# Row sums on quarters of the PE array, seven ring slots, and one kept weight chunk per layer

## The reference

```python
q = (xb @ w_query).reshape(PEER_BLOCK, PEER_HEADS, 2, D_HALF)
s = jnp.einsum('thpd,hpkd->thpk', q, sub_keys)
sv, si = lax.top_k(s, TOPK_HALF)                       # 16 best keys on each side
cand = sv[:, :, 0, :, None] + sv[:, :, 1, None, :]
cv, ci = lax.top_k(cand.reshape(...), TOPK)            # 16 best pairs
idx = i1 * N_KEYS + i2
g = jax.nn.softmax(cv, axis=-1)
a = jax.nn.gelu(jnp.einsum('thkd,td->thk', expert_u[idx], xb))
return jnp.einsum('thk,thkd->td', g * a, expert_v[idx])
```

## Time and profile before

| | |
|---|---|
| median of 3 runs | 1833.76 us |
| the profiled execution | 1834.33 us |
| its span, first to last instruction | 1832.5 us |
| mean granted TensorE clock | 0.967 |
| PE busy | 1557.9 us, 85% |
| DVE busy | 1268.3 us, 69% |
| POOL busy | 654.4 us, 36% |
| ACT busy | 287.1 us, 16% |
| DMA | 735.00 MB, mean 401 GB/s |
| chain that ended last | PE 44%, DMA 38%, DVE 8%, issue 7% |

### The profile page before, as it was taken

The page is one execution under the profiler, slowest core; times in us unless marked ns, Lnnn a source line. Parts: engine busy times, 40 slices in busy tenths (PEclk is TensorE's granted clock), DMA queues, the critical chain, the costliest instruction groups (busy, mean ns, idle before and its releaser), DMA issues.

```text
span 1832.5 us, 17962 instructions
## 1 busy us (share of the span) xinstructions
PE 1557.9 (85%) x5880; PEld 852.7 (47%) x5880; DVE 1268.3 (69%) x3220; ACT 287.1 (16%) x959; POOL 654.4 (36%) x580
## 2 busy tenths in 40 slices
PE   7987999998967999987778799989877778777776
PEld 6984566654823765642221177547423222222211
DVE  1338667867779667678887646676888976565565
ACT  1112131103112111111111111031111110000010
POOL 0012333334333233334444333353544443434441
PEclk9998999998988999999999999999999999999999
DMA  8779999999999999999999999999999999999996
GB/s 342 283 264 422 377 395 418 388 415 420 418 416 399 421 421 421 421 421 420 419 403 384 421 421 421 421 411 421 406 421 408 420 422 421 421 422 415 416 415 251
DMA packets 103536, 735.00 MB, mean 401 GB/s; under 512 B 12337, under 2 KB 12849, under 8 KB 14962
## 3 DMA queue, kind: packets, MB, share of 16 engines
q0 software_dynamic: 82944, 604.02, 80.1%
q1 hardware_dynamic: 19730, 127.92, 17.4%
q10 hardware_dynamic: 768, 1.91, 0.3%
HBM read 732.28 MB, written 1.52 MB: 400 GB/s over the span
## 4 chain that ended last, share of the span: by engine, by line
PE 44%; DMA 38%; DVE 8%; issue 7%; DVEq 2%; POOL 1%; ACT 1%; ACTq 0%; POOLq 0%
DMA uvring<-expert_uv_dram,idx 36%; PE psum L598 22%; PE psum L608 12%; PE psum L712 4%; PE psum L640 3%; DVE diag L1101 1%; DVE uvring L1088 1%; PE psum L616 1%; POOL uvring L565 1%; DMA arena<-ln_bias_dram 1%; DMA wring<-w_chunks_dram 1%; PE psum L733 1%; PE psum L692 1%; PE psum L695 1%; PE psum L630 0%
## 5 line engine op out<-in xcount | busy, mean ns | idle before, releaser
L598 PE MATMUL psum<-uvring,diag 128*128 128x512 f32 (+1 forms) x2160 | 1056.4, 626 | 250.7 <-DVE diag L1101 241.7
L565 POOL DMA_INDIRECT uvring<-expert_uv_dram,idx x576 | 654.2, 1136 | 1152.1 <-PE psum L598 967.9
L1088 DVE SCALAR_TENSOR_TENSOR uvring<-uvring,xn 128x1024 f32<-128x1024 f32 x576 | 705.1, 1224 | 377.2 <-DMA uvring<-expert_uv_dram,idx 365.6
L598 PEld LDWEIGHTS psum<-uvring,diag 128*128 128x128 f32 (+1 forms) x2160 | 375.3, 187 | 855.2 <-DVE diag L1101 482.8
L608 PEld LDWEIGHTS psum<-xT,wring 128*128 128x128 f32 x2304 | 296.6, 193 | 30.0 <-issue 28.4
L608 PE MATMUL psum<-xT,wring 128*128 128x160 f32 (+1 forms) x2304 | 300.2, 289 | 0.9 <-ACT xT L781 0.7
L844 ACT ACTIVATE a_gelu<-a_raw 128x1 f32<-128x1 f32 x576 | 114.8, 202 | 1169.9 <-DVE uvring L1088 1169.3
L1101 DVE TENSOR_SCALAR diag<-ident,a_gelu,gate 128x128 f32<-128x128 f32 x476 | 163.6, 344 | 34.6 <-ACT a_gelu L844 34.6
L763 ACT ACTIVATE arena<-psum 128x128 f32<-128x128 f32 (+2 forms) x164 | 48.6, 306 | 268.3 <-PE psum L608 177.4
L712 PE MATMUL psum<-wring,arena 128*128 128x256 f32 x384 | 88.1, 385 | 1.0 <-issue 0.8
L712 PEld LDWEIGHTS psum<-wring,arena 128*128 128x128 f32 x384 | 72.8, 192 | 18.7 <-issue 8.8
(11 more groups left out here) (93 smaller groups left out, 666.0 us busy)
## 6 DMA issues: line engine op xcount, KB each, us to landing
wring<-w_chunks_dram SPq DMA_DIRECT2D x106, 1024.0 KB
uvring<-expert_uv_dram,idx POOLq DMA_INDIRECT x576
uvring<-w_chunks_dram SPq DMA_DIRECT2D x6, 1024.0 KB, 12.5
gain<-gains_dram SPq DMA_DIRECT2D x4, 512.0 KB, 11.7
x<-x_tok_dram SPq DMA_DIRECT2D x2, 512.0 KB, 4.9
uvring<-ln_gain_dram SPq DMA_DIRECT2D x1, 1024.0 KB, 25.0
uvring<-ln_bias_dram SPq DMA_DIRECT2D x1, 1024.0 KB, 27.7
keys<-sub_keys_dram SPq DMA_DIRECT2D x2, 512.0 KB, 7.2
```

The source lines that it names most:

```text
L565: pool.indirect_dma_start(uvring[:, n % RING, :], None, expert_uv, bass.IndirectOffsetOnAxis(ap=idx[t][:, i:i + 1], axis=0),).then_inc(uv_ ...
L598: mm = nc.tensor.matmul(acc[0:r, c * 512:(c + 1) * 512], diag[:, place % DIAGS, 0:r], uvring[:, n % RING, D + c * 512:D + (c + 1) * 512], ...
L1088: nc.vector.scalar_tensor_tensor(out=uvring[:, slot, 0:D], in0=uvring[:, slot, 0:D], scalar=1.0, in1=xn[t][:, :], op0=ALU.mult, op1=ALU.mu ...
```

## The change

Row sums. For tiles 0 and 1 the product of a 128x128 diagonal with 128x512 becomes four products per item of 64x64 with 64x512: partition half i of the diagonal and of the v row, column half c, output on partition half j of bank i. Each of the four touches another quarter of the PE array. The diagonal is stored 64 wide (`twin`, made once, has the identity's two diagonal blocks side by side on the partitions). For tile 2 it is four products of 128x32 with 256 columns each, outputs on four strips of 32 partitions. `acc` then has half of the result on the wrong partitions, so at a tile's end a new ACT step, `turn_sum`, copies these parts to `turned` on the right ones, and `add_sum` adds from there.

Items on DVE. `ON_VECTOR` is empty; all 576 items go through PE.

Buffers. `RING` goes from 8 to 7. A new buffer `kept` holds the first chunk of each layer from the first pass to the second, so that it isn't loaded again; the other chunks go through `wring` as before. Five chunks instead of six lie in the expert ring at the start.

```diff
+KEEP = 1
+EARLY = KEEP + 5
+RINGED = [n for n in range(EARLY, PASS_CHUNK0[-1]) if n - max(p for p in PASS_CHUNK0 if p <= n) >= KEEP]
-RING = 8
+RING = 7
-ON_VECTOR = {(0, 0): (32, 128, (2, 6, 10, 14)), (1, 0): (0, 64, (3, 8, 13))}
+ON_VECTOR = {}
...
+                if c < KEEP:
+                    if n == PASS_CHUNK0[2] + c:
+                        unused(PASS_CHUNK0[1] + c)
+                        sp.dma_start(kept[:, c, :, :], w_chunks[LAYER_CHUNK0[1] + c]).then_inc(kept_landed[c], 16)
+                    return
...
-                for c in range(2):
-                    mm = nc.tensor.matmul(acc[0:r, c * 512:(c + 1) * 512], diag[:, place % DIAGS, 0:r],
-                                          uvring[:, n % RING, D + c * 512:D + (c + 1) * 512],
-                                          start=(n == mine[0]), stop=(n == mine[-1]))
+                if t == 2:
+                    for q in range(4):
+                        mm = nc.tensor.matmul(acc[32 * q:32 * q + 32, 0:256], diag[:, place % DIAGS, 0:32],
+                                              row[:, D + 256 * q:D + 256 * (q + 1)], start=first, stop=last)
+                else:
+                    for c in range(2):
+                        for i in range(2):
+                            j = i if c == 0 else 1 - i
+                            mm = nc.tensor.matmul(acc[64 * j:64 * j + 64, 512 * i:512 * (i + 1)],
+                                                  diag[64 * i:64 * i + 64, place % DIAGS, :],
+                                                  row[64 * i:64 * i + 64, D + 512 * c:D + 512 * (c + 1)],
+                                                  start=first, stop=last)
...
+            def turn_sum(l, t):
+                act.wait_ge(v_tensor, RANK[TENSOR_ITEMS[l, t][-1]] + 1)
+                if list(END).index((l, t)):
+                    act.wait_ge(acc_read, list(END).index((l, t)))
+                if t == 2:
+                    for q in range(1, 4):
+                        done = nc.scalar.copy(turned[0:32, 256 * (q - 1):256 * q], acc[32 * q:32 * q + 32, 0:256])
+                else:
+                    nc.scalar.copy(turned[0:64, 0:512], acc[64:P, 0:512])
+                    done = nc.scalar.copy(turned[64:P, 0:512], acc[0:64, 512:D])
+                done.then_inc(acc_turned, 1)
...
-                did(nc.vector.tensor_tensor(x[t][0:r, 0:512], x[t][0:r, 0:512], acc[0:r, 0:512], ALU.add))
-                nc.vector.tensor_tensor(x[t][0:r, 512:D], x[t][0:r, 512:D], acc[0:r, 512:D], ALU.add
+                if t == 2:
+                    did(nc.vector.tensor_tensor(x[2][0:32, 0:256], x[2][0:32, 0:256], acc[0:32, 0:256], ALU.add))
+                else:
+                    for i in range(2):
+                        rows = slice(64 * i, 64 * i + 64)
+                        did(nc.vector.tensor_tensor(x[t][rows, 0:512], x[t][rows, 0:512],
+                                                    acc[rows, 512 * i:512 * (i + 1)], ALU.add))
+                dve.wait_ge(acc_turned, list(END).index((l, t)) + 1)
+                r, s = (slice(0, 32), slice(256, D)) if t == 2 else (slice(0, P), slice(512, D))
+                nc.vector.tensor_tensor(x[t][r, s], x[t][r, s], turned[r, 0:D - s.start], ALU.add
                                         ).then_inc(acc_read, 1)
```

More of the change, by code:

```diff
@@ L464, in trunk @@
         w_landed = [sem(f"w_landed{r}") for r in range(WRING)]
-        early_landed = [sem(f"early_landed{c}") for c in range(EARLY)]
+        early_landed = [sem(f"early_landed{c}") for c in range(EARLY - KEEP)]
+        kept_landed = [sem(f"kept_landed{c}") for c in range(KEEP)]
         part_used = sem("part_used")
@@ L478, in trunk @@
         v_tensor, v_vector, acc_read = sem("v_tensor"), sem("v_vector"), sem("acc_read")
+        acc_turned = sem("acc_turned")
         y_ready, conv_ready = sem("y_ready"), sem("conv_ready")
@@ L485, in early_chunk @@
         def early_chunk(c):
-            return uvring[:, 2 + c, :].rearrange("p (k c) -> p k c", k=KD)
+            return uvring[:, 2 + c - KEEP, :].rearrange("p (k c) -> p k c", k=KD)
         def wait_group(e, key):
@@ L501, in load_chunk, with unused @@
                 l = 0 if n < PASS_CHUNK0[2] else 1
-                c, r = n - max(p for p in PASS_CHUNK0 if p <= n), n - EARLY
-                if r >= WRING:
-                    kind, what = CHUNK_AFTER[n - WRING]
+                c = n - max(p for p in PASS_CHUNK0 if p <= n)
+                def unused(m):
+                    kind, what = CHUNK_AFTER[m]
                     if kind == "part":
@@ L512, in _ @@
             sp.dma_start(ident[:, :], ident_c).then_inc(ident_landed, 16)
-            for c in range(EARLY):
-                sp.dma_start(early_chunk(c), w_chunks[c]).then_inc(early_landed[c], 16)
+            for c in range(KEEP):
+                sp.dma_start(kept[:, c, :, :], w_chunks[c]).then_inc(kept_landed[c], 16)
+            for c in range(KEEP, EARLY):
+                sp.dma_start(early_chunk(c), w_chunks[c]).then_inc(early_landed[c - KEEP], 16)
             for n in range(EARLY, EARLY + WRING):
@@ L581, in chunk @@
             def chunk(n, c):
+                if c < KEEP:
+                    pe.wait_ge(kept_landed[c], 16 * (n // 2 + 1))
+                    return kept[:, c, :, :]
                 c += PASS_CHUNK0[n]
                 if c < EARLY:
-                    pe.wait_ge(early_landed[c], 16)
+                    pe.wait_ge(early_landed[c - KEEP], 16)
                     return early_chunk(c)
-                r = c - EARLY
+                r = RINGED.index(c)
                 pe.wait_ge(w_landed[r % WRING], 16 * (r // WRING + 1))
@@ L592, in weigh @@
                 l, t, _ = ITEMS[n]
-                mine, place, r = TENSOR_ITEMS[l, t], RANK[n], 32 if t == 2 else P
+                mine, place = TENSOR_ITEMS[l, t], RANK[n]
+                first, last, row = n == mine[0], n == mine[-1], uvring[:, n % RING, :]
                 if n == mine[0] and (l, t) != (0, 0):
@@ L852, in _ @@
                     gelu(2 * p + 1)
+                for lt, end in END.items():
+                    if p == end + 1:
+                        turn_sum(*lt)
                 for k in PLAN["ACT"].get(p, []):
@@ L1138, in _ @@
             dve.wait_ge(const_landed, 16 * N_CONST)
+            after(did(nc.vector.tensor_tensor(twin[:, :], ident[:, 0:64], ident[:, 64:P], ALU.add)))
             for p in range(TURNS):
```

17 lines of the change are left out of this document (11 added, 6 removed).

## The result

The changed kernel takes 1820.94 us (median of 4 runs, 1820.36 to 1821.85), the kernel before 1832.78 (4 runs, 1831.26 to 1833.84). The ratio is 0.9939, 95% interval 0.9924 to 0.9955: 11.8 us faster, where 9.2 had been forecast. The profiled execution took 1821.85 us, its span is 1820.0.

The account below looks back on a forecast made before the run. DMA was taken to bound the kernel, with one of 16 engines lagging. Terms -5.0 - 5.8 + 2.0 + 1.3 - 1.7 = -9.2 us gave 1825 us, forecast 1816 to 1830 (chance 0.52), range 1813 to 1842.

Parts of the forecast that it names:

- Bytes: DMA reads: two of 112 weight chunks of 1 MB are no longer read, -5.0 us (-2.5 if the first met gaps).
- PE products: Pass 1 of layer 0: four products side by side, row-sum pair 1.9 us instead of 3.70, DMA leads: -5.8 us.
- The 36 items on DVE: Row sums moved to PE: DVE loses 46 us but idles for DMA in the pure stretches, counted as 0.
- Rival E: Faster: DVE's 46 us also count and more of the DMA shortfall returns; 1809 us, chance 0.10.
- The ring of seven: Gather slots: one fewer cuts the landing reserve from 7.8 to 5.3 us; +2.0 us, bounds 0 and +20.
- Rival B: Tile ends, routing steps and start: seven slots drain at bursts, +20 in place of +2; 1843 us, chance 0.11.
- PE's fetches: Instruction fetching: 4896 more PE instructions, 19 more packets spread over 16 DMA engines, +1.3 us.
- Rival A: PE's instruction fetches hit the DMA engine that is behind: +18 in place of +1.3; 1842 us, chance 0.10.
- The tail: Kernel's end, last data to last add: 3.25 us after instead of 4.97 before, -1.7 us.
- The laggard: One of 16 DMA engines, about six us behind, ends every gather; each q14 packet costs it 0.95 us.
- C: Gains cancel: PE overlaps by two only and the slot reserve costs 5 us; 1833 us, chance 0.14.
- D: Row sums on PE: no products overlap, 3.44 us per row; about 2290 us, chance 0.03.

Follow-up runs that it names:

- e2: The changed kernel without the kept chunk (new sums, seven slots, both first chunks loaded twice): 1827.08 us, ratio 0.9973 to the kernel before.
- e4: The changed kernel with the 36 items added by DVE again: 1824.27 us, ratio 0.9952 to the kernel before.
- e1: The changed kernel with eight slots and no kept chunk, so the new sums and empty ON_VECTOR alone: 1823.57 us, ratio 0.9953 to the kernel before.
- e3: The changed kernel with the old row sums and the 36 items on DVE, still seven slots and the kept chunk: 1851.27 us, ratio 1.0100 to the kernel before.
- e7: The changed kernel with each item's four products issued twice, the second time with zero weights: 1874.41 us, ratio 1.0234 to the kernel before.
- e9: The changed kernel with products issued twice (second time zero weights), eight slots and no kept chunk: 1858.19 us, ratio 1.0137 to the kernel before.
- e6: The changed kernel with four one-column zero-weight products more on PE per item of tiles 0 and 1: 1821.33 us, ratio 0.9944 to the kernel before.
- e5: The changed kernel with four one-element memsets more on DVE behind each dot (2304 more instructions): 1841.76 us, ratio 1.0056 to the kernel before.
- e10: The changed kernel with the diagonals made on ACT right behind each gelu, not on DVE: 1812.05 us, ratio 0.9886 to the kernel before.
- e12: The kernel of e10 with two one-element memsets more on DVE behind every dot (1152 more instructions): 1821.22 us, ratio 0.9936 to the kernel before.
- e11: The changed kernel with six slots instead of seven, still one kept chunk: 1847.00 us, ratio 1.0074 to the kernel before.

## Why the prediction was right, and where its sizes were off

Sign and mechanism held, and the time lay 4 us under the forecast of 1825: 2.6 of it are gain that was not forecast, 1.0 that the kernel before took 1832.78 and not 1833.76, the rest rounding. That the total came so near is in part luck, since terms missed in both directions. Step by step:

- **Bytes**, -5.0: measured -6.1 by the medians (e2 to the changed kernel), -2.6 from the first gather on. Right within what the runs can tell.
- **PE products**: four side by side, the pair at 1.95 us for 1.9 forecast, pass 1 at 411 GB/s for "410 or more", PE 88% busy for "below 90%". The rate alone gives 13/421 of 229 us, 7.1 us, where 5.8 was put. Measured for the new sums as a whole, the 36 items with them: -9.2 (-8.0 from the first gather on), against -5.8 + 1.3 - 1.7 = -6.2.
- **The 36 items on DVE**, 0: this is the term that failed. They were worth some 3.3 us (e4), as much as the difference between 9.2 and 6.2, though no run shows that it is the same 3 us. I argued from the stretch of gathers alone, where DVE idles; the items lay in stretches with routing and dense work. Rival E may have had the mechanism, but at 20 us it was far too large.
- **The ring of seven**, +2.0: measured +3.5 by the medians (e1, e2), 0 from the first gather on. Its bound of +20 belonged to another kernel: with the old sums it is 18.5 to 24.6 (e3), with doubled ones 16.2 to 22.3 (e7, e9). Rival B's mechanism is real, and the new sums are what keeps it away. I had summed the slot and the products as terms that add, and they don't: e1 alone is -9.2, the slot and the chunk under the old sums are +18.5, and all three together are -11.8, not +9.3.
- **PE's fetches**, +1.3: 31 more packets cost 0.4 us (e6), so it is nearer 0. Rival A is refuted.
- **The tail**, -1.7: measured 6.47 - 5.69 = 0.8 us less. I took PE at full clock, 1.1 us for two items by my estimate; the granted clock was 0.50 and they took 1.93. One item of tile 2 takes 0.64 us at a clock of 1.00 (at 966.24 us of the changed kernel) and 1.08 at 0.50 (at 962.80).
- **Changes of tile size on PE.** The rows show a small price, which the forecast had left out. In the kernel before, the record of a dense block L640 is 3.72 us long right behind the strips of L616 and 3.62 behind the full-array sums; that of the sums is 3.60 behind L640 and 3.70 behind strips:

```profile
209.83 3.72 PE L640 MATMUL psum<-wring,xT 128*128 128x256 f32 x16
213.38 3.60 PE L598 MATMUL psum<-uvring,diag 128*128 128x512 f32 x8
```

In the changed kernel the dense block behind the 64x64 sums is 3.72 us long (at 184.39, above). By the starts, the new turn is 1.88 + 3.65 + 1.00 = 6.53 us, the old one 3.54 + 3.54 + 1.00 = 8.08. The old turn has two changes of tile size (128x128 to 128x32 and back), the new one three, since the sums are 64x64. Eight old matmuls at 0.43 take 3.44 us; half of that saved would leave 6.36. So the third change costs 0.17 us per turn at most, an estimate from these rows.

- **The laggard.** The claim that one DMA engine sets the end, and that DVE's packets on q14 cost it 0.95 us each, stood on two waits in a trace. It predicted +17 for e5 (measured +20.8), -7.6 for e10 (-8.9) and +8.6 for e12 (+9.2). Which of the 16 engines it is, and why DVE's fetches fall on it, no run shows. The prediction's books don't close either: two of the 47 packets fall ahead of 130 us, the other 45 make 43 us at 0.95, and the stalls and the lead of the other engines were put at 34.
- **Not forecast:** the first gather was issued 1.85 us sooner, at 128.50 and not at 130.35. In the profiles of the other kernels, which have the same work ahead of it up to the order of a load, it came anywhere from 125.79 to 130.39, so I don't count it to the change. From the first gather on the two profiled executions differ by 10.6 us.

C and D are out: at a granted clock of 1.00 the sixteen records took 1.95 us, and the gains did not cancel. (D's own sum, 512 x 3.44 + 500, is 2261 and not 2290, which changes nothing.)

## What to carry to other kernels

A buffer's price is not a number of its own: from eight to seven slots it was 0 to 3.5 us or 18.5 to 24.6, by how long the slowest user held a slot, so shorten the hold before taking the buffer, and price both edits together. When all DMA engines look full and the end is still late, look at the period of the long waits: if it is one instruction packet of one engine, moving that engine's small instructions to another that idles can be worth more than its busy time says (here 8.9 us, e10, with DVE busy 67% of the span). And look for what an engine's spare time is worth in the stretch where the edit lies, not in the one where the engine idles most.

## What the hardware showed that I had not expected

- Instruction packets have very different prices: one of DVE's about 0.9 us of the kernel's time (9.2 us for ten in e12), ACT's none that shows (e10), PE's of 16 KB 0.4 us for 31 (e6). DVE's and ACT's are counted on one queue: q14 grew by 10 packets with 1152 more DVE instructions (e12 against e10) and by 4 with 1152 more on ACT and 576 fewer on DVE (e10).
- PE's mean granted clock is 0.79 in the changed kernel, 0.97 before and 0.93 with doubled products (e7, e9), so the slower clock belongs to the faster kernel. In the stretch of gathers alone it is 0.63 and PE is busy 164 of 235 us, 70%, where I had forecast about 40%. A cost of it shows only in the tail, 0.8 us against my estimate at full clock; what it costs the kernel elsewhere no run tests.
- The last slots are not worth the same: the eighth 3.5 us at most, the seventh 26, with landing times of about 14, 11.5 and 9 us after the issue for eight, seven and six slots (e1, the changed kernel, e11).
- The stretch up to the first gather, the same work in five of the kernels, took from 125.79 to 129.81 us: differences of 2 or 3 us between two kernels need more than their medians.
